# Gate pieces between the steps of the delta rule: four behind every second step pair in place of two or four by the kind of step

## The reference, cut to what matters

```python
    decay = jnp.exp(jnp.where(tril, gc[..., :, None] - gc[..., None, :], NEG_INF))
    kb = k * beta[..., None]
    vb = v * beta[..., None]
    lmat = jnp.where(strict, jnp.einsum('bhncd,bhnsd->bhncs', kb, k) * decay, 0.0)
    eye = jnp.eye(CHUNK, dtype=jnp.float32)
    rhs = jnp.concatenate([vb, kb * jnp.exp(gc)[..., None]], axis=-1)
    sol = lax.linalg.triangular_solve(lmat + eye, rhs, left_side=True, lower=True, unit_diagonal=True)
    ...
    attn_intra = jnp.einsum('bhncd,bhnsd->bhncs', q, k) * decay
```

```python
    z = gdn_z.reshape(bn, seq_len, GDN_HEADS, GDN_HEAD_DIM).astype(jnp.float32)
    o_gdn = (rms_norm(o_gdn, gdn_norm_w) * jax.nn.silu(z)).astype(h.dtype).reshape(bn, seq_len, GDN_WIDTH)
    ...
    gate = jax.nn.sigmoid(gates.astype(jnp.float32) + gate_bias.astype(jnp.float32)).astype(h.dtype)
```

## Time and profile before

| | before |
|---|---|
| median of 3 runs | 2835.96 us (2828.89 to 2838.26) |
| profiled execution | 2823.42 us |
| its span in the profile | 2822.1 us |
| mean granted clock of TensorE | 0.981 |
| TensorE busy | 2705.8 us, 96% |
| VectorE, ScalarE, GpSimd busy | 57%, 37%, 23% |
| stage of the change | from 1986 to 2238 us of the span |

### The profile page before, as it was taken

The page is one execution under the profiler, slowest core; times in us unless marked ns, Lnnn a source line. Parts: engine busy times, 40 slices in busy tenths (PEclk is TensorE's granted clock), DMA queues, the critical chain, the costliest instruction groups (busy, mean ns, idle before and its releaser), DMA issues. The chain is left out here.

```text
span 2822.1 us, 42499 instructions
## 1 busy us (share of the span) xinstructions
PE 2705.8 (96%) x16586; PEld 2320.4 (82%) x16586; DVE 1598.9 (57%) x2482; ACT 1053.2 (37%) x1827; POOL 642.0 (23%) x509
## 2 busy tenths in 40 slices
PE   8989999999999999998999999999899989999998
PEld 6769876788888777877888888986799889999987
DVE  5875657366653455954533337965544465666643
ACT  4364333442222333353423224546434243422223
POOL 3440101221100123441100003346344320112101
PEclk9999899999999999999999999999999999999999
DMA  4200231122222321312222222210111032222221
GB/s 163 92 8 8 91 104 60 46 90 97 97 97 97 117 75 62 103 38 74 92 97 97 97 97 76 87 50 1 51 35 46 28 120 85 88 91 91 97 98 60
DMA packets 64276, 219.08 MB, mean 78 GB/s; under 512 B 8182, under 2 KB 8822, under 8 KB 63830
## 3 DMA queue, kind: packets, MB, share of 16 engines
q1 hardware_dynamic: 61190, 211.62, 22.3%
q10 hardware_dynamic: 2896, 4.82, 0.5%
HBM read 210.07 MB, written 6.32 MB: 77 GB/s over the span
## 5 line engine op out<-in xcount | busy, mean ns | idle before, releaser
L308 PE MATMUL ps<-normed,slab_parts 128*128 128x512 f32 (+3 forms) x2280 | 789.8, 346 | 23.7 <-DVE normed L646 10.1
L310 PE MATMUL ps<-normed,slab_parts 128*128 128x512 f32 (+3 forms) x2280 | 767.8, 337 | 0.0
L309 PE MATMUL ps<-normed,slab_parts 128*128 128x512 f32 (+3 forms) x2280 | 767.3, 337 | 0.0
L163 ACT ACTIVATE slab_parts<-ring 128x1024 fp32r<-128x1024 f32 x360 | 380.1, 1057 | 893.3 <-PE ps L310 876.6
L167 DVE TENSOR_TENSOR slab_parts<-ring,slab_parts 128x1024 fp32r<-128x1024 f32 x344 | 461.5, 1344 | 380.7 <-ACT slab_parts L163 380.3
L308 PEld LDWEIGHTS ps<-normed,slab_parts 128*128 128x128 f32 x2280 | 434.3, 190 | 78.0 <-issue 20.0
L309 PEld LDWEIGHTS ps<-normed,slab_parts 128*128 128x128 f32 x2280 | 434.5, 191 | 47.3 <-issue 5.3
L310 PEld LDWEIGHTS ps<-normed,slab_parts 128*128 128x128 f32 x2280 | 433.7, 190 | 44.4
L308 PE MATMUL ps<-hidden,slab_parts 128*128 128x512 f32 x560 | 219.5, 392 | 5.6 <-DVE hidden L258 5.6
L310 PE MATMUL ps<-hidden,slab_parts 128*128 128x512 f32 x560 | 219.3, 392 | 0.0
L309 PE MATMUL ps<-hidden,slab_parts 128*128 128x512 f32 x560 | 219.3, 392 | 0.0
(11 more groups left out here) (602 smaller groups left out, 4351.1 us busy)
## 6 DMA issues: line engine op xcount, KB each, us to landing
ring<-in_stream SPq DMA_DIRECT2D x376, 512.0 KB, 3.3
scratch_gates<-fox_y SPq DMA_DIRECT2D x12, 258.0 KB, 2.3
branch_gates<-scratch_gates ACTq DMA_DIRECT2D x1, 2064.0 KB, 15.1
h<-in_x SPq DMA_DIRECT2D x8, 256.0 KB, 5.3
scratch_fox_y<-fox_y SPq DMA_DIRECT2D x1, 1032.0 KB, 6.8
gdn_z<-scratch_gates ACTq DMA_DIRECT2D x1, 1032.0 KB, 5.1
fox_y<-scratch_fox_y ACTq DMA_DIRECT2D x1, 1032.0 KB, 17.2
mix_y<-in_sgu_b SPq DMA_DIRECT2D x1, 1024.0 KB, 6.6
```

Of the source, the lines that this page charges most:

```text
L163: self.nc.scalar.activation(self.hi[:, n % PARTS, :], self.ring[:, n % SLOTS, :], ACT.Copy).then_inc(self.hi_ready, 1)
L308: nc.tensor.matmul(to, lhsT[0], rhs[0], start=start, stop=False)
L309: nc.tensor.matmul(to, lhsT[0], rhs[1], start=False, stop=False)
L310: return nc.tensor.matmul(to, lhsT[1], rhs[0], start=False, stop=stop)
```

## The change

The table `room` no longer looks at the steps: behind every odd step pair stand four pieces, behind an even one none.

```diff
         for n in range(LAST + APART):
             steps = [(n - q * APART) % STEPS for q in range(2) if 0 <= n - q * APART < LAST]
             slot += len(steps)
-            room[slot - 1] = 2 + 2 * (TRIANGLE in steps) - 2 * (PAIRS in steps)
+            room[slot - 1] = 4 * (n % 2)
         woven = weave(room)
```

## The result

The changed kernel takes 2847.28 us in the median of 7 runs (2838.82 to 2855.0), the kernel before on the same chip 2832.47 (7 runs, 2825.24 to 2838.26). The ratio is 1.0055, 95% interval 1.0039 to 1.0071: 0.55%, some 15.6 us, slower (the two medians lie 14.8 apart). The forecast was a change of +10.8 and a time of 2846.8.

What follows compares the result with a forecast made beforehand. TensorE's own queue was taken to bound the stage, so its uncovered waits count whole. 7.7 + 0.8 + 2.7 + 1.0 + 1.2 - 2.6 = +10.8 us on 2835.96 gave 2846.8, range 2838 to 2859.

Steps and rivals of the forecast that it cites:

- pairs 7 to 9: Four pieces ahead of L3925 no longer cover the waits of L3912 and L3900: 1.53 us a chunk, 7.7 in five.
- first chunk and first pairs: In the first chunk L3900 comes hardly later, but two pieces fewer lie before it and follow behind: 0.8 us.
- pairs 10 and 11: Short cover between add and product, and VectorE late at L3980: 0.45 us a chunk, 2.7 in six.
- pairs 1 and 2: A moved L192 between L3964 and L3980 makes L3912 wait: 0.2 us a chunk, 1.0 in five.
- tail: From pair 96 on, pairs 96 and 98 lose their two pieces, so adds follow products directly: 1.2 us.
- visits: Gate-piece visits fall from 85 to 48, each saving 0.07 us: -2.6 us.
- Rival C: Faster: dearer visits saved and TURN's chain starting at PAIRS, L3960 before pair 8's L3980; -9.7 us, 2826; chance 0.05.
- the grant stays 1.00 in the stage: Sign in the profile after: TensorE's granted clock does not fall inside the changed stage; a fall would make the forecast wrong.
- rival B: The clock falls at six places of close waits, 10.2 us in all: +21, or 2857 us; chance 0.10.
- Rival A: Order costs less, within 0.3%: VectorE not late at pairs 2 and 11, dear visits saved; +5.7, 2842; chance 0.21.
- both terms of VectorE: VectorE's lateness at pairs 10 and 11 (2.7 us) and at pairs 1 and 2 (1.0 us).
- D: Nothing is seen: the stage's loss is given back behind it and the time stays at 2836 us; chance 0.08.

Runs made afterwards that it cites:

- only visits joined: Kernel before, with the two pieces of pairs 4, 12 and 14 moved to pairs 5, 13 and 15, saving 18 visits: 2837.83 us, one run.
- six pieces: Kernel before, with the two pieces of pairs 4 and 12 moved to pairs 0 and 8: 2825.28 us, ratio 0.998.
- only the middle moved: Kernel before, with only the four pieces behind pair 8 moved to behind pair 7: 2840.65 us, ratio 1.0029.

## Why the prediction was right, and where it was not

The kernel became slower by the mechanism that was forecast, and the time of 2846.8 lies 0.5 beside the measured median. Part of that is luck: the runs beside which it was measured have a median 3.5 below the 2835.96 from which I started, and the change is +15, not +10.8. What held is the sum of the waits. Without its falls of the clock (1.5, 2.1 and 0.7) the stage would be 11.7 us longer, for a forecast of 10.8; the falls, which the sum has at nothing, are the rest. By terms, in the stage:

| term | forecast, us | measured, us |
|---|---|---|
| pairs 7 to 9, chunks 2 to 6 | 7.7 | 7.15 |
| first chunk and first pairs | 0.8 | 2.3, with a fall |
| pairs 10 and 11 | 2.7 | 3.7 |
| pairs 1 and 2 | 1.0 | 1.0 |
| tail | 1.2 | 1.2 |
| visits | -2.6 | -2.3 |
| end of the stage, a fall | 0 | 0.7 |
| falls behind pair 9 | 0 | 2.1 |
| sum | 10.8 | 15.9, of 16.0 |

The terms are sums of rounded times, so 0.1 us more or less means nothing. The two falls stand at 1.05 each, net of what the wait at pair 11 gives back.

**Pairs 7 to 9** held. L3912 waits 0.76 (forecast 0.82) and L3900 1.47 (1.5), 2.23 in place of 0.80: 1.43 a chunk for 1.53. Moving those pieces alone showed the same waits, and putting them back took them away. Rival C needed L3960 to start ahead of that L3980; it starts behind it.

**The first chunk.** L3900 of pair 9 stands 24.91 behind the stage's start (2030.01 - 2005.10) instead of 23.36 (2014.06 - 1990.70): 1.55 later and not the 0.06 forecast; with the two pieces left behind (0.73) it is 2.3. What I missed is at pair 5. TensorE's timeline of the changed kernel:

```profile
2014.39 0.86 PE L3925 MATMUL ps<-gdn_prod,gdn_inv 128*88 128x88 f32 x8 [0.55 <-ACT gdn_prod L4012]
2016.47 0.51 PE L3912 MATMUL ps<-square_constants,gdn_invT 88*88 88x88 f32 x4 [1.22 <-DVE gdn_invT L3980]
2016.81 1.21 PE L3916 MATMUL ps<-gdn_invT,gdn_A_level 128*88 128x88 f32 x8
2017.74 0.56 PE L308 MATMUL ps<-gate_rows,slab_parts 128*128 128x258 f32 x1
...
2020.44 0.79 PE L3925 MATMUL ps<-gdn_prod,gdn_inv 128*88 128x88 f32 x8
```

Without the two pieces behind pair 4 the wait for VectorE stands open for 1.44, and the grant falls right after: L3916 takes 0.93 for 0.58 and the visit 2.70 for 1.53, together 1.5. Eleven profiles are of kernels without those pieces (eight kernels), and the wait stands open in all. In nine the grant falls right behind it; in the other two (only visits joined, six pieces) it fell already among the warm-up matmuls and stays at 1.00 behind the wait. The kernel before and the one with only the middle moved keep the pieces and show no fall here. So the open wait goes with the fall but isn't enough for it, and no run filled it.

**Pairs 10 and 11** were under-sized, 0.62 a chunk for 0.45; 0.10 of it is the change of shape from 88 to 32 rows, which stood in a gate visit before. L3980 starts 3.04 behind L3900 (forecast 3.0), but by way of two L192 in 2.15 and not 1.50. The Trainium skill (SBUF — State Buffer, "Who interferes with whom") says of VectorE and GpSimd on their shared ports that whoever issues first holds them for its whole instruction and the other waits. The trace agrees for L192, which reads two tiles of SBUF: its pair takes 2.15 us for 0.8 beside two GpSimd operations, and ends at 2074.98, behind the end of the second, at 2074.70.

**Pairs 1 and 2, the tail, the visits** came as forecast. At pair 2 of the second chunk, after:

```profile
2053.35 0.47 PE L3900 MATMUL ps<-square_constants,gdn_inv 88*88 88x88 f32 x4
2053.94 0.29 PE L3912 MATMUL ps<-square_constants,gdn_invT 32*32 32x32 f32 x4
```

0.59 from one to the other, and before 0.40 (2035.21 to 2035.61): 0.19 a chunk. In the tail the first of the two naked pairs, after:

```profile
2256.57 0.79 PE L3916 MATMUL ps<-gdn_invT,gdn_A_level 128*88 128x88 f32 x8
2257.91 0.86 PE L3925 MATMUL ps<-gdn_prod,gdn_inv 128*88 128x88 f32 x8 [0.55 <-ACT gdn_prod L4012]
```

1.34 where 0.58 are work, and in the second (32 rows) 0.79 where some 0.37 are: 0.76 and 0.42. The gate matmuls take 4.5 us less in 48 visits than in 85, but some 2.2 of it return in the steps, which now change shape by themselves: -2.3.

**The clock** is the step that failed: "the grant stays 1.00 in the stage". I had set rival B against 20 us with long waits and a full grant, and gave it 0.10 as six falls behind pair 9, 10.2 us. The runs show two of them in each profile of the change, of 1.1 us each and not 1.7, besides one in the first pairs (1.5) and one at the stage's end (0.7). B's mechanism was real, but worth 2.1 of its 10.2 us at its own place. I had also written that by a rule of the Trainium skill (TensorE: Matmul & The Clock Gate, "HAM oscillation — how this bites in real kernels") waits that a product splits in two leave the clock alone; here the grant fell behind such waits. The Trainium skill tells elsewhere (TensorE: Matmul & The Clock Gate, "A second HAM failure mode: psum-queue depth-cycling") of a kernel in which frequent short idles between groups of matmuls make the clock go up and down. The filled waits agree with that section: with the idles taken away, two falls behind pair 9 in each of three profiles became none in two. It does not tell why four of six such places keep the clock, nor does any run.

**Rival A** (within 0.3%) fell with its condition, as both terms of VectorE were 4.7 together and not under 1.5 (3.4 without the change of shape and the short cover). **D** fell too: 15.9 of the 18.1 us between the second profile of the change and the one before lie in the stage, and nothing behind gives them back.

## What to carry to other kernels

Filler work belongs where the engine that sets the end would wait; look up the longest chain from its last issue to the next thing it needs, and put in as much filler as that chain has room (here six pieces behind pair 8 and two behind pair 0, which made a kernel faster than both). An even spread by count costs the same work and leaves the chain bare. When a forecast opens new short waits on TensorE, price the clock as well: run the kernel once with the waits filled by idle matmuls, which parts the two losses. Then compare chunk by chunk, and not only the whole stage: a fall of the clock at another place, as at the stage's end here, would be counted with the ones in question.

## What the runs showed of the hardware

- Waits of 0.76 and 1.47 us (1.14 in the first chunk) with 0.94 us of matmuls between them were followed by a fall of the granted clock to 1.2 GHz for 3.4 us in two of six places in each of three profiles of the change. A fall cost 1.5 us in slower matmuls, of which a later wait gave back 0.4. The same waits filled with idle matmuls: no fall behind them in two profiles. The same waits in other orders: none in one profile, with the other pieces spread as before, and one in another, with two pieces at pair 10. With VectorE's quarters later (0.76 and 1.13) there were two. So as far as these runs show, the waits are needed for it and do not suffice.
- Behind an open wait of 1.44 us in the first pairs came the same fall in nine of the eleven profiles of kernels without the pieces behind pair 4, at 1.5 us in the change. In the other two the clock had fallen already, 2.3 us behind the stage's start, and it stayed at 2.4 GHz behind the wait.
- Two 128x256 operations of VectorE on SBUF, 0.8 us alone, took 1.50 beside one operation of GpSimd and 2.15 beside two, while VectorE's L3970, L3762 and L3980, which read PSUM, kept their 0.4 to 0.5.
